# Scaling the expert outputs per slot, before they are stored, instead of per token at the end

## The reference, cut to what matters

```python
y = jnp.zeros((B * T, D), jnp.float32)
for e in range(N_EXPERTS):
    hid = jax.nn.silu(xt @ p['moe_w_gate'][e]) * (xt @ p['moe_w_up'][e])
    y = y + gates[:, e:e + 1] * (hid @ p['moe_w_down'][e])
...
x = x + gt2 * _moe(h, p)      # gt2: one modulation row for context, one for latent tokens
...
final: x * rsqrt(mean(x * x) + eps) * final_norm_w
```

## Time and profile before

| what | value |
|---|---|
| timed runs | 1041.52, 1044.01, 1037.5 us |
| profiled execution, time | 1032.39 us |
| profiled execution, span | 1030.7 us, granted TensorE clock 0.961 |
| PE busy | 927.8 us (90%) |
| DVE busy | 446.2 us (43%) |
| ACT busy | 257.2 us (25%) |
| POOL busy | 139.1 us (14%) |
| DMA | 192.60 MB, mean 187 GB/s |
| L1689 evictions on ACT, units of 3 tiles | x7, mean 811 ns |

### The profile page before, as it was taken

How to read it: one execution, slowest core, us unless ns; L and a number is a source line. 1 busy time by engine, 2 the same in 40 slices (tenths; PEclk the granted TensorE clock), 3 DMA queues, 4 the chain that set the end, 5 groups by cost and what they waited for, 6 DMA issues and landing times.

```text
span 1030.7 us, 23771 instructions
## 1 busy us (share of the span) xinstructions
PE 927.8 (90%) x10741; PEld 650.1 (63%) x10741; DVE 446.2 (43%) x739; ACT 257.2 (25%) x437; POOL 139.1 (14%) x162
## 2 busy tenths in 40 slices
PE   4899998879999999998999899988999999999940
PEld 4445576756665546798999754567777856665510
DVE  3255567984444435457666632546101010100047
ACT  4346242332113256222222311220001111101003
POOL 6000000000004002456336000000100000000031
PEclk9999999999999999999999899978999999999975
DMA  9840009663203900300000248153699999999945
GB/s 337 312 164 4 1 24 333 220 230 105 75 13 105 325 7 1 105 3 22 3 3 23 98 169 327 62 183 124 243 363 380 405 401 374 405 390 387 403 150 199
DMA packets 55902, 192.60 MB, mean 187 GB/s; under 512 B 7486, under 2 KB 10964, under 8 KB 51700
## 3 DMA queue, kind: packets, MB, share of 16 engines
q1 hardware_dynamic: 42096, 161.09, 41.5%
q0 software_dynamic: 6992, 22.85, 6.8%
q10 hardware_dynamic: 6708, 7.07, 2.0%
HBM read 168.27 MB, written 22.73 MB: 185 GB/s over the span
## 4 chain that ended last, share of the span: by engine, by line
PE 77%; DVE 11%; ACT 4%; DMA 4%; issue 3%; DVEq 0%; ACTq 0%; POOL 0%; SPq 0%; POOLq 0%
PE ps L748 18%; PE ps L1239 14%; PE ps L1262 7%; PE ps L1052 7%; PE ps L1105 7%; PE ps L1040 4%; PE ps L738 4%; PE ps L1009 3%; DMA ring<-in_moe_w_up 2%; PE ps L852 2%; PE ps L904 2%; PE ps L763 1%; PE ps L1173 1%; PE ps L1155 1%; DMA arena<-in_x_sample 1%
## 5 line engine op out<-in xcount | busy, mean ns | idle before, releaser
L748 PE MATMUL ps<-hT,ring 128*128 128x128 f32 x704 | 193.6, 434 | 3.5 <-ACT hT L1355 3.5
L748 PEld LDWEIGHTS ps<-hT,ring 128*128 128x128 f32 x704 | 104.9, 191 | 84.0 <-issue 76.2
L2501 DVE TENSOR_TENSOR hT<-ps,hT 128x384 f32<-128x384 f32 (+3 forms) x18 | 9.1, 506 | 234.6 <-ACT hT L1678 224.3
L1239 PE MATMUL ps<-ring,arena 128*32 128x128 f32 (+3 forms) x1104 | 86.0, 370 | 2.8 <-DVE arena L2467 1.6
L1239 PEld LDWEIGHTS ps<-ring,arena 128*32 128x32 f32 (+1 forms) x1104 | 60.0, 116 | 28.5 <-issue 21.6
L1841 POOL DMA_INDIRECT arena<-h_rows,slot_tok x18 | 16.6, 920 | 371.4 <-PE ps L738 208.0
L1239 PE MATMUL ps<-arena 128*32 128x256 f32 (+2 forms) x1056 | 60.8, 387 | 1.1 <-DVE arena L2467 1.1
L738 PE MATMUL ps<-ident,arena 128*128 128x128 f32 (+3 forms) x316 | 44.5, 288 | 15.0 <-DMA arena<-in_x_sample 10.4
L1239 PEld LDWEIGHTS ps<-arena 128*32 128x32 f32 x1056 | 46.7, 112 | 15.8 <-issue 2.9
L738 PEld LDWEIGHTS ps<-ident,arena 128*128 128x128 f32 (+3 forms) x316 | 39.5, 177 | 22.0 <-issue 18.0
L2236 DVE TENSOR_TENSOR arena<-arena,ps 128x512 f32<-128x512 f32 x50 | 34.4, 687 | 32.3 <-PE ps L1052 31.4
(11 more groups left out here) (452 smaller groups left out, 1471.2 us busy)
## 6 DMA issues: line engine op xcount, KB each, us to landing
ring<-in_ada_w SPq DMA_DIRECT2D x12, 2048.0 KB, 12.6
ring<-in_moe_w_gate SPq DMA_DIRECT2D x7, 2048.0 KB, 9.5
arena<-in_moe_w_gate SPq DMA_DIRECT2D x7, 2048.0 KB, 10.2
arena<-in_moe_w_up SPq DMA_DIRECT2D x7, 2048.0 KB, 14.9
arena<-in_moe_w_down SPq DMA_DIRECT2D x7, 2048.0 KB, 20.4
ring<-in_moe_w_up SPq DMA_DIRECT2D x7, 2048.0 KB, 15.7
ring<-in_moe_w_down SPq DMA_DIRECT2D x7, 2048.0 KB, 21.5
ring<-in_w_in SPq DMA_DIRECT2D x6, 2048.0 KB, 9.3
```

The source lines that it names most:

```text
L748: last = mm(out, w[:, k, cols], hT[:, k, a:b], start=(k == 0), stop=(k == KD - 1))
L1239: last = mm(ps[rows_of(n, g), GU, 512 * i + at:512 * i + at + width], m_xgT[:, b % 2, k, rows_of(n, j)], w[:, k, col:col + width], start=( ...
```

## The change

- DVE computes the gates `gw` before the one-hots, and a second block one-hot that is multiplied by the gate of the token. The products of `slots` so have 64 columns instead of 32: the token of each slot, and its gate.
- `spread_slots`: eight small products with parts of the identity bring the pair (token, gate) of each slot to the partitions on which the folded outputs of that slot lie. DVE makes two weights of each slot: the gate if the token is a context one, else zero, and the reverse (`slot_weights`).
- `factors(b)`: DVE builds for unit b a tile `m_fac`: context row times first weight plus latent row times second weight, in two operations for a unit of 4 tiles, four for 2, eight for 3 and for 1.
- `scaled(b)`: DVE evicts the down product times `m_fac` in place of ACT's copy; ACT still issues the stores.
- In the tail DVE adds first rows and second rows straight to `x_rows`; both scalings (L2516, L2548) go.
- POOL reads the table once and puts all optional work, the repeat of the first gathers too (with a new list `slot_late`), behind one jump, ahead of its wait for the last store.
- ACT executes one Sqrt on a single column ahead of the tail.

The core of the diff:

```diff
@@ POOL
-            over_blocks(pool, gather)
+            over = pool.value_load(table[0:1, MAX_OVER:MAX_OVER + 1], min_val=0, max_val=MAX_OVER)
+            with pool.If(over > 0):
+                ...
             stored(NU - 1)
-
-            over_blocks(pool, stored)
...
-            any_over(pool, first_rows_again)
             outputs(m_yB, slot[:, 1, :], ys_dram, s_y_in)
@@ ACT
-                act.wait_ge(block_full[DN], b + 1)
-                if b >= 2:
-                    act.wait_ge(s_ys_stored[b % 2], stores(b - 2))
-                A(m_dn[:, b % 2, 0:256 * n], ps[:, DN, 0:256 * n], ACT.Copy).then_inc(block_free[DN], 1)
                 act.wait_ge(block_free[DN], b + 1)
...
+            ch(A(small[:, 61:62], small[:, 1:2], ACT.Sqrt))
@@ PE
-                    last = mm(ps[:, HD, 512:512 + NB], m_hot_p[:, n, :], m_hot_b[:, n, :], start=(n == 0), stop=(n == 2 * NT - 1))
+                    last = mm(ps[:, HD, 512:512 + 2 * NB], m_hot_p[:, n, :], m_hot_b[:, n, :, :].rearrange("p i b -> p (i b)"),
+                              start=(n == 0), stop=(n == 2 * NT - 1))
...
+            def spread_slots():
+                rows = m_raw[:, 0, :, :].rearrange("p i b -> p (i b)")
+                at = lambda a: slice(512 + 2 * NB * a, 512 + 2 * NB * a + 2 * NB)
+                pe.wait_ge(s_tok, 2)
+                for g in range(2):
+                    mm(ps[64 * g:64 * g + 64, HD, at(1)], ident[:, 0:64], rows, start=True, stop=True)
+                for g in range(4):
+                    last = mm(ps[32 * g:32 * g + 32, HD, at(2)], ident[:, 0:32], rows, start=True, stop=True)
+                for j in (1, 2):
+                    last = mm(ps[96:P, HD, at(2 + j)], ident[:, 32 * j:32 * j + 32], rows, start=True, stop=True)
+                last.then_inc(s_spread, 1)
@@ PE, in the loop over units, behind gathered(b + 1)
+                if b == 0:
+                    spread_slots()
@@ DVE
+            for c in range(2):
+                link(TT(out=m_cg[:, :, :], in0=m_t1[:, :, :], in1=wide(m_ab[:, c, :], 2, NE), op=ALU.is_equal))
+                link(TT(out=m_cg[:, :, :], in0=m_cg[:, :, :], in1=m_gate[:, :, :], op=MULT))
+                link(V.tensor_reduce(gw[:, c, :], m_cg[:, :, :], AX.X, ADD))
...
+            SCALE_PIECES = {1: [(slice(32 * g, 32 * g + 32), 0, 256 * g, 256, 2) for g in range(4)],
+                            2: [(slice(64 * g, 64 * g + 64), 0, 512 * g, 512, 1) for g in range(2)],
+                            3: [(slice(0, 96), 0, 0, 768, 0)] + [(slice(96, P), 256 * j, 768, 256, 2 + j) for j in range(3)],
+                            4: [(slice(0, P), 0, 0, D, 0)]}
...
+            def factors(b, ch=ch):
+                for rows, at, col, width, a in SCALE_PIECES[UNITS[b][1] if b < NU else 4]:
+                    out = m_fac[rows, at:at + width]
+                    ch(TS(out, m_gt[0][rows, col:col + width], m_w[rows, a, 0, b:b + 1], None, MULT))
+                    ch.sync()
+                    ch(STT(out=out, in0=m_gt[1][rows, col:col + width], scalar=m_w[rows, a, 1, b:b + 1], in1=out, op0=MULT, op1=ADD))
+                ch.sync()
+            def scaled(b):
+                n = 256 * (UNITS[b][1] if b < NU else 4)
+                dve.wait_ge(block_full[DN], b + 1)
+                if b >= 2:
+                    dve.wait_ge(s_ys_stored[b % 2], stores(b - 2))
+                TT(out=m_dn[:, b % 2, 0:n], in0=ps[:, DN, 0:n], in1=m_fac[:, 0:n], op=MULT).then_inc(block_free[DN], 1)
+                dve.wait_ge(block_free[DN], b + 1)
@@ DVE, in the loop over units: hidden(b), transposed(b + 1), [b == 0: slot_weights()], then
+                if b:
+                    scaled(b - 1)
+                factors(b)
+            scaled(NU - 1)
@@ DVE, tail
-                    link(STT(out=m_y[:, t, :], in0=m_y[:, t, :], scalar=gw[:, 0, t:t + 1], in1=m_gt[min(t, 1)], op0=MULT, op1=MULT))
-                    TT(out=m_y[:, t, :], in0=m_y[:, t, :], in1=x_rows[:, t, :], op=ADD).then_inc(s_yA, 1)
+                    TT(out=x_rows[:, t, :], in0=x_rows[:, t, :], in1=m_y[:, t, :], op=ADD).then_inc(s_yA, 1)
+                dve.wait_ge(s_yA, NT * n)
...
-                link(STT(out=m_yB[:, t, :], in0=m_yB[:, t, :], scalar=gw[:, 1, t:t + 1], in1=m_gt[min(t, 1)], op0=MULT, op1=MULT))
-                TT(out=m_x2[:, t, :], in0=m_yB[:, t, :], in1=m_y[:, t, :], op=ADD).then_inc(s_x2, 1)
+                TT(out=x_rows[:, t, :], in0=x_rows[:, t, :], in1=m_yB[:, t, :], op=ADD).then_inc(s_x2, 1)
```

More of the change, by code:

```diff
@@ L1722, in final_rms @@
                 r = small[:, 24 + t:25 + t]
-                ch(A(m_sq, m_x2[:, t, :], ACT.Square, accum_out=r))
+                ch(A(m_sq, x_rows[:, t, :], ACT.Square, accum_out=r))
                 ch.sync()
@@ L1862, in _ @@
             pool.wait_ge(s_table, 1)
-            over_blocks(pool, gather)
-            stored(NU - 1)
-            over_blocks(pool, stored)
-            def first_rows_again():
-                pool.wait_ge(s_yA, NT)
-                outputs(m_y, slot[:, 0, :], ys_dram, s_yA_in)
-            any_over(pool, first_rows_again)
+            over = pool.value_load(table[0:1, MAX_OVER:MAX_OVER + 1], min_val=0, max_val=MAX_OVER)
+            with pool.If(over > 0):
+                with ExitStack() as nest:
+                    for j in range(MAX_OVER):
+                        nest.enter_context(pool.If(over > j))
+                        gather(NU + j)
+                stored(NU - 1)
+                with ExitStack() as nest:
+                    for j in range(MAX_OVER):
+                        nest.enter_context(pool.If(over > j))
+                        stored(NU + j)
+                pool.wait_ge(s_yA, NT)
+                outputs(m_y, slot_late, ys_dram, s_yA_in)
+            stored(NU - 1)
             outputs(m_yB, slot[:, 1, :], ys_dram, s_y_in)
@@ L2473, in _ @@
             ch(V.tensor_reduce(pair_of(m_blk), m_ge[:, :, 1:NB + 1], AX.X, ADD))
-            link(TT(out=m_hot_b[:, :, :], in0=m_ge[:, :, 0:NB], in1=m_ge[:, :, 1:NB + 1], op=SUB))
+            link(TT(out=m_hot_b[:, :, 0, :], in0=m_ge[:, :, 0:NB], in1=m_ge[:, :, 1:NB + 1], op=SUB))
             ch(STT(out=pair_of(m_in), in0=pair_of(m_blk), scalar=-float(P), in1=pair_of(m_sf), op0=MULT, op1=ADD))
+            link(TT(out=m_hot_b[:, :, 1, :], in0=m_hot_b[:, :, 0, :], in1=wide(pair_of(gw), 2, NB), op=MULT))
             for c in range(2):
-                ch(TT(out=m_hot_b[:, NT * c:NT * c + NT, :], in0=m_hot_b[:, NT * c:NT * c + NT, :],
+                ch(TT(out=m_hot_b[:, NT * c:NT * c + NT, 0, :], in0=m_hot_b[:, NT * c:NT * c + NT, 0, :],
                       in1=wide(num[:, 16:16 + NT], 2, NB), op=MULT))
@@ L2490, in _ @@
             TS(table[:, 0:MAX_OVER + 1], m_of[:, 0:MAX_OVER + 1], float(NE - 1), None, MIN).then_inc(s_table, 1)
[L2492 to L2495, removed]
             def hidden(b):
@@ L2521, in over, with first_rows @@
                 hidden(b)
-            def first_outputs_again():
+                factors(b, over_chain)
+                scaled(b)
+            def first_rows(n):
                 for t in range(NT):
-                    dve.wait_ge(s_yA_in[t], 32)
-                    STT(out=m_y[:, t, :], in0=m_y[:, t, :], scalar=gw[:, 0, t:t + 1], in1=m_gt[min(t, 1)],
-                        op0=MULT, op1=MULT).then_inc(s_yA_again, 1)
-                    dve.wait_ge(s_yA_again, t + 1)
-                    TT(out=m_y[:, t, :], in0=m_y[:, t, :], in1=x_rows[:, t, :], op=ADD).then_inc(s_yA, 1)
-                dve.wait_ge(s_yA, 2 * NT)
-            dve.wait_ge(s_fin_in, 48)
-            first_outputs()
+                    dve.wait_ge(s_yA_in[t], 16 * n)
+                    TT(out=x_rows[:, t, :], in0=x_rows[:, t, :], in1=m_y[:, t, :], op=ADD).then_inc(s_yA, 1)
+                dve.wait_ge(s_yA, NT * n)
+            first_rows(1)
             dve.wait_ge(s_table, 1)
             over_blocks(dve, over)
-            any_over(dve, first_outputs_again)
+            any_over(dve, lambda: first_rows(2))
             def final_norm(t):
@@ L2541, in final_norm @@
                 link(V.reciprocal(small[:, 24 + t:25 + t], small[:, 24 + t:25 + t]))
-                STT(out=m_out[:, t, :], in0=m_x2[:, t, :], scalar=small[:, 24 + t:25 + t], in1=m_fw,
+                STT(out=m_out[:, t, :], in0=x_rows[:, t, :], scalar=small[:, 24 + t:25 + t], in1=m_fw,
                     op0=MULT, op1=MULT).then_inc(s_out, 1)
-            dve.wait_ge(s_yA, NT)
             for t in range(NT):
                 dve.wait_ge(s_y_in[t], 16)
-                link(STT(out=m_yB[:, t, :], in0=m_yB[:, t, :], scalar=gw[:, 1, t:t + 1], in1=m_gt[min(t, 1)], op0=MULT, op1=MULT))
-                TT(out=m_x2[:, t, :], in0=m_yB[:, t, :], in1=m_y[:, t, :], op=ADD).then_inc(s_x2, 1)
+                TT(out=x_rows[:, t, :], in0=x_rows[:, t, :], in1=m_yB[:, t, :], op=ADD).then_inc(s_x2, 1)
                 if t:
```

32 lines of the change are left out of this document (24 added, 8 removed).

## The result

Nine timed runs of each: after 1029.45 us in the median (1026.24 to 1036.48), before 1036.06 (1033.27 to 1044.01). The medians lie 6.6 us apart, the means (1037.88 and 1029.85) 8.0. The ratio, which goes by all runs, is 0.9923, 95% interval [0.9893, 0.9952]: 0.77% or 8.0 us faster, and surely faster, with 4.9 to 11.0 us inside the interval. The two profiled executions are only 2.5 us apart (spans 1030.7 and 1028.2), so where the time went has to be read in three stretches. The page's busy times after, to be set beside the table of before: DVE has 60.7 us more, ACT 12.9 less.

A forecast was written before the change was run, and what follows sets the result against it. PE and the weight stream bound the units, DVE the tail. The tail's 8.0 us less 0.3 for early products gave 7.7, taken off a median of 1041.52 us: 1033.8, with 8 in 10 between 1029 and 1038.5.

The forecast's parts named there:

- The tail's 8.0: Tail without scaling: second rows start 1.7 us sooner and their phase is 6.3 us shorter, 8.0 us saved.
- the last one: Closing step on chances: 1% is 10.4 us, about what measurement can tell; faster by over 1% 0.16, within 0.80, slower 0.04.
- Second phase 13.9 us: Second rows in the tail: 13.9 us from first addition to last norm's end, where it was 20.2; saves 6.3.
- The gather starts the phase, DVE is ready first: Tail: DVE is ready for second rows at 1004.4 us, before the first second gather lands at 1005.7.
- Phase start 1.7 sooner: Tail: second rows begin when their first gather lands at 1005.7 us, 1.7 us before the old 1007.39.
- POOL 0.8 us from landing to issue: Tail: POOL issues the first second gather 0.8 us after the last store lands, where it took 2.1.
- Rival (c): Tail: the last store lands early, in 2.4 us; gain 9.2 us, time 1032.3 us; chance 0.08.
- Early products 0.3: Slot-weight and spreading products on PE, ahead of unit 1's gate products, cost 0.3 us, bounds 0 to 1.1.
- Table load near 995: ACT's table load (1.28 us) is done near 995 us, where ACT has nothing to do, before the second rows.
- Units cost nothing: Units: DVE's evictions and factors (2.0 to 4.0 us a unit) fit under PE's gate and up products; no cost.
- (d): Units: narrow factor pieces cost 1.5 us each instead of 0.4 and delay following units; 16 us lost, 1050 us; chance 0.03.
- Rival (a): Tail: DVE's jump over optional blocks takes 3.4 us, as long as PE's; gain 5.7 us, 1035.8 us; chance 0.09.

The follow-up runs named there:

- g0: Kernel before, with DVE's two table reads and jumps made one read and one jump ahead of the first-row additions; 1035.65 us, ratio 0.9996.
- g1: e1 with DVE's reads and jumps made one read and one jump ahead of the first-row additions; 1036.45 us, ratio 1.0000 to the kernel before.
- e1: Changed kernel with the old tail on DVE and POOL and without ACT's early Sqrt; 1041.1 us, ratio 1.0033 to the kernel before.
- a_again: The changed kernel measured again, unaltered; 1032.60 us, ratio 0.9952 to the kernel before.
- e3: Changed kernel with the factors built once, for one unit, and used for all units; 1029.34 us, ratio 0.9923 to the kernel before.
- e2: Kernel before with the new tail (additions only), POOL's single jump and ACT's early Sqrt; 1028.6 us, ratio 0.9907 to the kernel before.
- e8: Changed kernel with DVE's two reads and jumps made one read and one jump ahead of the first-row additions; 1030.14 us, ratio 0.9920.
- h1: e8 measured again, unaltered; 1028.29 us, ratio 0.9904 to the kernel before.
- h2: h1 with DVE building every unit's factors twice, the same values; 1026.75 us, ratio 0.9892 to the kernel before.
- h4: h1 without ACT's early Sqrt; 1026.22 us, ratio 0.9909 to the kernel before.
- h3: h1 with POOL's old three table reads and jumps, two of them behind the last store's landing; 1030.51 us, ratio 0.9939 to the kernel before.
- g2: e2 with DVE's reads and jumps made one read and one jump ahead of the first-row additions; 1027.15 us, ratio 0.9908 to the kernel before.

## Why the prediction was right and wrong

Tail lengths, read from the timelines of all kernels:

| kernels | from the eviction of the last unit but one to the end, us | from the last eviction, us |
|---|---|---|
| before | 45.7 | 38.0 |
| g0, g1 (old tail, jump ahead) | 45.8, 45.6 | 39.8, 39.5 |
| e1 (old tail, late instructions) | 50.6 | 44.4 |
| after, a_again, e3 | 37.3, 38.5, 37.3 | 31.2, 32.4, 31.1 |
| e2 (new tail alone, jump behind) | 38.0 | 32.0 |
| e8, h1, h2, h4 | 36.8, 35.3, 35.8, 36.4 | 30.7, 29.2, 29.7, 30.2 |
| h3 (POOL's old jumps) | 37.7 | 31.6 |
| g2 (new tail alone, jump ahead) | 36.0 | 30.0 |

**The gain and its place: right.** 7.7 us were forecast; 8.0 were measured (6.6 between the medians), 5 in the second measurement of the same kernel (0.9952). The tail's 8.0 stands against 8.4 in the profile and 8.0 by the table (45.7 less 37.7, the mean of after, a_again and e3). That the two profiles are only 2.5 us apart is the clock and the scatter ahead of the units, and not the change. That the tail's sum came out so near is in part luck, for two terms missed in opposite ways. Counted from the eviction of the last unit but one, the second phase starts 3.0 us sooner where 1.7 were forecast, as the slow last product of before (1.7 us) stood in the path that the forecast followed; and the phase is 5.3 us shorter where 6.3 were forecast, as DVE's idle time came in.

**The step that failed is the last one: "One per cent is 10.4 us, about what a measurement of this kernel can tell from no change".** It rested on three runs that lie 6.5 us apart. With nine runs of each kernel the half-width of the interval is 0.3%, so a gain of 0.7% is a faster kernel and not "no change", and the chances (0.80 within 1%) put nearly everything on the reading that nothing can be told, where the sum of the prediction itself said 7.7 us with only a few small terms against it. Its own 1% went unquestioned.

**The base was off as well.** The median of the three runs, 1041.52, is 5.5 us above that of nine (1036.06); the other chips gave 1037.5, 1037.3 and 1036.9. The profile's 1032.39 was below that. "No row says where those 9 us are" was true, and 7.7 off 1036.06 is 1028.4, which is 1 us from the result. So 1033.8 was 4.3 us too high while the difference was right; the range held 1029.45 at its very edge.

**Term by term.**
- *Second phase 13.9 us*: 13.6 to 14.0 in e8, h1, h2; 14.9 in after and 15.8 in a_again, as DVE's idle time behind the jump came in. Period 2.53 us, as forecast.
- *The gather starts the phase, DVE is ready first (1004.4 against 1005.7)*: wrong. After, the landing was at 1009.90 and DVE's jumps ended at 1010.33. Counted from the last eviction the landing came after 12.9 us (forecast 13.0) but DVE's readiness after 13.3 (forecast 11.7). The 1.6 us came from the profile of before: its last product ran partly at the lower clock (5.34 for 3.64 us), so its last eviction was late and its first gathers stood 3.4 us ahead of it, where it is 1.7 after (and 0.8 in g0, the same units without that stretch). From that profile the order of the two looked safer than it was. In e2 and e3 DVE comes last without any doubt: its second additions wait for nothing but its own two reads and jumps.
- *Phase start 1.7 sooner*: from the last eviction 14.7 us before and 13.3 after, 1.4; with the jump ahead 12.3 to 13.5.
- *POOL 0.8 us from landing to issue*: 0.3, and h3 shows the jumps' share to be 1.9 where 1.3 was assumed. Rival (c) did not come: the last store took 6.2 us to land.
- *Early products 0.3*: nothing. *Table load near 995*: 1000.51, still off the path.
- *Units cost nothing*: right, by 281.50 us for the old and for the new ones, and by g1 against g0 and h2 against h1 as far as times can tell. The pieces took 0.35 and 0.48 us where 0.4 was assumed. What cover there is was never used up even at twice the factors, so (d) falls.

**Rival (a) was half right.** Its price was copied from PE (3.38 us) and its row, the jump, was the wrong place to look: DVE's jump took 72 and 56 ns after as well. The idle time comes a few instructions later: 1.7 us in after, 2.6 in a_again, some 3 beyond the jumps' own 2.3 in e1, none in e3 and e2. The Trainium skill (Runtime: NRT & Kernel Launch, Instruction fetch mechanics) says that a taken branch whose target lies outside the window of two blocks forces a fetch before execution goes on; I had taken from it that a jump of some 210 instructions is free. The runs decide: it isn't always free, even at the same size of the optional blocks: e3 has those of the changed kernel, fewer instructions ahead of them, and no idle time of this kind. That the fetch is what DVE waits for is argued and not shown, and the packets of the instruction queue fit it only in part (e3 has one too); shown is that the idle time goes with the edit that puts the jump ahead. Which layout of the code brings it is open, since no view shows where an instruction lies in its block.

**The best version** is the changed kernel with DVE's jump ahead. Its tail is 1.9 us shorter than that of the changed kernel by the table (e8 and h1 36.1 on average, after and a_again 37.9). Its two measurements are 0.9920 and 0.9904 against 0.9923 and 0.9952; the four intervals overlap, so the times alone only point that way.

## What to carry to other kernels

Work that fits under a saturated PE is free even in amounts that look large (twice 49 us of factors beside 250 us of products cost nothing that could be measured here), so move it off a serial tail; then look for what else stood on that tail. Put conditional jumps, and reads of registers from memory, where the engine waits anyway: the jump's own duration is not its price, the idle time of the operations behind it is. Before two profiles are compared, look for the products at which the granted clock was low: here they, and not the change, made the units look 1.5 us slower. And decide from the spread of repeated runs what "no change" means, before you put a chance on it: a sum of 7.7 us is not no change if the runs can be repeated.

## What was not expected of the hardware

- A jump of 56 ns was followed by idle time of DVE, right behind it (4.4 us in e1) or one operation later (1.7 and 2.6 us), which ended 1.7 to 1.9 us after a packet of the instruction queue; in before, e2 and e3, with the jump at the same place, there was none.
- Short stretches at the lower clock (0.5) turn up in the units in ten of the fourteen profiles, at changing places. One costs up to 1.7 us where it falls on products (5.34 for 3.64 us, 12.35 for 10.69), and it shifts the order of things behind it. The five looked at closely (712 and 948 us in after, 724 and 988 in before, 906 in e3) stood behind an idle time of PE of 1.05 to 2.9 us.
- Two profiles of the same kernel differ by 2.1 us in when the units start (705.02 and 707.12) and by 4.3 in how long they take (285.8 and 281.5 to the last unit but one), of which 3.1 are two stretches at the lower clock. A difference of a few microseconds between two single profiles can only be read within a stretch whose start is tied to the same event.
